# Sixteen small bias transfers in place of one, a private bias buffer, and a reordered program start in a two-block transformer kernel

## The chip, the cores and the metric

The kernel runs on one core of a Trainium2 chip, as one program in one launch. The metric is the device time of that program in microseconds (us), of which lower is better. Times are medians over runs; the spread of the runs is given beside them. The profile is that of one further execution.

The engines are named as in the profile: PE is TensorE, DVE VectorE, ACT ScalarE, POOL GpSimd and SP SyncE. SP and POOL only issue transfers here. The transfers of all queues are carried out by the core's 16 DMA engines.

## The reference

The input is x, 256 tokens by 1024 features, in fp32. It goes through two blocks of two layers each. The first block is an "even" mixer (sparse and compressed attention), an MLP, a differential-attention mixer (the second mixer, called DIFF or "d" in the code) and an MLP, and ends in a norm. The second block is a pooling mixer, an MLP, a block attention with a relative-position bias (MOBA or "b") and an MLP, all with norms that are scaled and shifted by vectors computed from an input c. What the change touches is the start of the first layer and the bias of the last attention:

```python
def rms_norm(x, g):
    y = xf * lax.rsqrt(jnp.mean(xf * xf, axis=-1, keepdims=True) + NORM_EPS)
    return (y * g.astype(jnp.float32)).astype(x.dtype)
...
# first block
u = rms_norm(h, mix_norm_g[layer])
h = h + even_mixer(u, even_w_in[e], ...)          # proj = u @ w_in, rope, attentions, @ w_out
...
# second block, layer 1 (moba_attention)
bias_own = rb[t5_bucket(jnp.maximum(dist_own, 0))].transpose(2, 0, 1)[None]
logit_own = jnp.einsum('bhqd,bhkd->bhqk', qf, k_own) * scale + bias_own
logit_own = jnp.where((dist_own >= 0)[None, None], logit_own, -jnp.inf)
```

The bias depends on the distance between query and key only, so one row of 384 values for each of the 16 heads holds all of it.

## The kernel before

**Tiling.** Tokens lie in two tiles of 128 (t = 0, 1). All weights come from one array, in_stream, cut into 179 pieces of up to 128 x 2048 fp32 (1024 KB). SP loads piece n into raw[n % 4]. ACT copies it to whi in a shortened format (L416, or L586 in halves), DVE subtracts to get the rest, wlo (L700, or L811 in halves), and PE multiplies both parts with the split activations uh and ul (L1216), three matmuls for one product. The even mixer's first two pieces are 128 x 1392 (the values, L1495), and its pieces 2 to 7 are features, which are turned by rope: DVE multiplies by sine and cosine (L863, L864), PE adds the swapped half (L1518), ACT copies out to qk (L535).

**What sets the order.** Every engine runs a list written out by hand; semaphores join them. SP issues piece n + 4 when wlo of piece n is done (`lo_ready`, L342). ACT and DVE follow tables that say at which quarter of which piece a step is done. In the second mixer ACT begins piece i + 3 in quarter 1 of piece i and DVE finishes piece i + 2 in quarter 3 (hi_beside, lo_beside). The semaphore `used` counts pieces that PE has finished: DIFF is 42 (the second mixer's first piece), MLP1 is 58 (the first piece of the MLP after it).

**The start.** SP issues the two halves of x and then the first four pieces. ACT issues the constants con (2197 columns) on its own DMA queue. The norm of tile t is: square and sum (L426), square root (L431), scaling on DVE (L733), transposes on PE (L1294), gain on ACT (upper, L443), split into uh and ul on DVE (lower, L746, L747). Then come the values of the even mixer. ACT does whi of pieces 0 and 1 ahead of the gain of both tiles; DVE does wlo of both ahead of both splits.

**The bias rows.** PE gathers the bias rows into a bank (L1662), right after the first feature piece. DVE adds the mask and writes them to gb (L889), which is a view of PT, the buffer of transposed attention weights: 16 partitions by 384 values. POOL then sends gb to bias_rows in device memory, each row 128 times, with a pitch of 512 values (L365). ACT waits for that transfer (L506) before it goes on to piece 4, since it will write PT later. Much later, ahead of the last attention, POOL reads the rows back, shifted by one for each partition, into hank, 16 transfers (L398).

**POOL's list** is: small inputs, the bias rows, eight copies of the compressed keys (L372, L373), two copies of keys (L376, L377), and three times 16 pieces of w_mod (1024 KB each, L391) that DVE reduces beside the MLPs. The second 16 wait for `used` at the end of the second mixer and are used in the MLP after it.

## Time and profile before

| | us |
|---|---|
| median of 3 runs | 1263.24 |
| lowest, highest | 1263.09, 1263.97 |
| the profiled execution | 1265.12 |
| its span in the trace | 1263.2 |
| PE busy (share of the span) | 1155.1 (91%) |
| DVE busy | 807.2 (64%) |
| ACT busy | 592.3 (47%) |
| POOL busy | 45.7 (4%) |

The profiled execution took 1.9 us more than its span and 1.9 us more than the median of the runs. PE is the busiest engine by far, so what matters are the stretches in which it does not work, or works at the lower of its two clocks. The granted mean clock is 0.966 of full speed. In the span cut into 40 equal slices PE is at 4, 1 and 6 tenths in the first three and at 9 in nearly all others; the slices with low PE are those of the start, of the pooling mixer (slices 23 and 24) and the very end.

### The profile page before, as it was taken

Reading aid. Unit: us, or ns where it says so; the run is one execution under the profiler, and the core shown is the slowest. Engines: PE = TensorE matmul, PEld = TensorE weight load, DVE = VectorE, ACT = ScalarE, POOL = GpSimd, SP = SyncE. Lnnn points to the kernel's source line nnn. Section 1 sums busy time; section 2 is a strip of 40 time slices with the busy share of each in tenths; the row PEclk is TensorE's granted clock in tenths of the full one; section 3 lists DMA queues with packets and bytes.
Section 4 is the critical chain, followed back from the end, with each engine's and each line's share of the span. In section 5 each row is a group of like instructions: output and inputs, shape, how many; then the busy total and the mean of one; then the engine's idle time right before and its main releaser. Section 6 shows DMA issues by size and latency. Waiting matters only on the chain.

```text
span 1263.2 us, 18055 instructions
## 1 busy us (share of the span) xinstructions
PE 1155.1 (91%) x7384; PEld 1015.3 (80%) x7384; DVE 807.2 (64%) x1287; ACT 592.3 (47%) x914; POOL 45.7 (4%) x88
## 2 busy tenths in 40 slices
PE   4169999999999999899999849999999998999997
PEld 4167675999998877699999649999978987999996
DVE  4035734787777666787777686877775556655554
ACT  5023534634445556564344545444446454644342
POOL 1010000000000000000000000000002000000000
PEclk9679999999999999999999969999999999999999
DMA  7852403797773433569777334977735434455530
GB/s 267 122 138 71 167 27 149 297 354 276 272 293 134 167 104 130 200 254 351 276 273 277 119 133 155 359 276 279 298 134 180 154 133 150 168 199 180 187 134 34
DMA packets 35810, 248.57 MB, mean 197 GB/s; under 512 B 4304, under 2 KB 4320, under 8 KB 6928
## 3 DMA queue, kind: packets, MB, share of 16 engines
q1 hardware_dynamic: 26352, 188.61, 40.3%
q0 software_dynamic: 9232, 57.69, 13.8%
q8 instruction: 59, 0.97, 0.3%
q10 hardware_dynamic: 144, 1.12, 0.2%
q14 instruction: 23, 0.19, 0.0%
HBM read 242.55 MB, written 4.19 MB: 195 GB/s over the span
## 4 chain that ended last, share of the span: by engine, by line
PE 80%; DVE 9%; ACT 4%; issue 4%; DMA 3%; POOL 0%; DVEq 0%; ACTq 0%; POOLq 0%
PE bank L1216 67%; DMA bias_rows<-PT 3%; PE bank L1398 2%; PE bank L1632 2%; PE bank L1423 1%; DVE wlo L700 1%; PE bank L1615 1%; ACT vo L426 1%; DVE x L720 1%; DVE wlo L811 1%; PE bank L1447 1%; PE bank L1446 1%; PE bank L1445 1%; DVE work L718 1%; PE bank L1696 1%
## 5 line engine op out<-in xcount | busy, mean ns | idle before, releaser
L700 DVE TENSOR_TENSOR wlo<-raw,whi 128x2048 fp32r<-128x2048 f32 (+2 forms) x143 | 324.6, 2274 | 138.0 <-ACT whi L416 137.9
L1216 PE MATMUL bank<-uh,whi 128*128 128x256 f32 x1272 | 369.6, 291 | 36.4 <-ACT vo L522 36.4
L1216 PE MATMUL bank<-ul,whi 128*128 128x256 f32 x1272 | 361.4, 284 | 0.0
L1216 PE MATMUL bank<-uh,wlo 128*128 128x256 f32 x1272 | 361.4, 284 | 0.0
L416 ACT ACTIVATE whi<-raw 128x2048 fp32r<-128x2048 f32 (+2 forms) x143 | 270.5, 1896 | 38.9 <-DMA bias_rows<-PT 37.8
L1216 PEld LDWEIGHTS bank<-uh,whi 128*128 128x128 f32 x1272 | 245.4, 193 | 44.8 <-issue 42.5
L1216 PEld LDWEIGHTS bank<-ul,whi 128*128 128x128 f32 x1272 | 245.5, 193 | 4.4 <-issue 2.2
L1216 PEld LDWEIGHTS bank<-uh,wlo 128*128 128x128 f32 x1272 | 245.2, 193 | 0.0
L1216 PE MATMUL bank<-whi,hh 128*128 128x512 f32 x544 | 214.0, 393 | 0.0
L1216 PE MATMUL bank<-wlo,hh 128*128 128x512 f32 x544 | 212.4, 390 | 0.0
L1216 PE MATMUL bank<-whi,hl 128*128 128x512 f32 x544 | 211.8, 389 | 0.0
L1216 PEld LDWEIGHTS bank<-whi,hl 128*128 128x128 f32 x544 | 102.1, 188 | 22.0
L1216 PEld LDWEIGHTS bank<-whi,hh 128*128 128x128 f32 x544 | 102.4, 188 | 20.5 <-issue 1.2
L1216 PEld LDWEIGHTS bank<-wlo,hh 128*128 128x128 f32 x544 | 102.4, 188 | 18.8 <-issue 0.2
L474 ACT ACTIVATE hh<-work 128x512 fp32r<-128x512 f32 x56 | 35.4, 632 | 173.3 <-PE bank L1216 173.3
L470 ACT ACTIVATE work<-bank 128x512 f32<-128x512 f32 x56 | 33.5, 598 | 174.0 <-PE bank L1216 174.0
L762 DVE CUSTOM_DVE_ANT_0 qk<-qk,cb 128x1024 f32<-128x1024 f32 x96 | 113.2, 1222 | 0.0
L1216 PE MATMUL bank<-whi,uh 128*128 128x256 f32 (+2 forms) x256 | 90.3, 353 | 19.8 <-DVE ul L747 10.5
L1216 PE MATMUL bank<-whi,ul 128*128 128x256 f32 (+2 forms) x256 | 86.8, 339 | 0.0
L1216 PE MATMUL bank<-wlo,uh 128*128 128x256 f32 (+2 forms) x256 | 86.7, 339 | 0.0
L776 DVE TENSOR_TENSOR work<-work 128x512 f32<-128x512 f32 x56 | 38.7, 691 | 74.5 <-ACT work L470 74.5
L1216 PEld LDWEIGHTS bank<-whi,uh 128*128 128x128 f32 x256 | 52.0, 203 | 26.7 <-issue 16.8
(211 smaller groups left out, 1185.7 us busy)
## 6 DMA issues: line engine op xcount, KB each, us to landing
raw<-in_stream SPq DMA_DIRECT2D x176, 1024.0 KB, 4.9
qk<-in_w_mod POOLq DMA_DIRECT2D x48, 1024.0 KB, 5.9
bias_rows<-PT POOLq DMA_DIRECT2D x1, 3072.0 KB, 33.0
u<-bias_rows POOLq DMA_DIRECT2D x16, 128.0 KB, 2.7
raw<-in_stream SPq DMA_DIRECT2D x2, 696.0 KB, 12.5
con<-in_con ACTq DMA_DIRECT2D x1, 1098.5 KB, 6.9
x<-in_x SPq DMA_DIRECT2D x2, 512.0 KB, 8.1
vo<-in_fin_g POOLq DMA_DIRECT2D x2, 512.0 KB, 4.9
```

Source lines behind the costliest of these rows:

```text
L416: nc.scalar.activation(whi[:, c % RING, 0:w], raw[:, n % RING, 0:w], ACT.Copy).then_inc(hi_ready, 1)
L426: nc.scalar.activation(o_[:, t, 512 * h:512 * h + 512], x[:, t, 512 * h:512 * h + 512], ACT.Square, accum_out=ss[:, 2 * t + h:2 * t + h + ...
L470: nc.scalar.activation(work[:, s % 2, :], bank[s % 2][:, :], ACT.Relu).then_inc(relu_done, 1)
L474: nc.scalar.activation(hh[:, s % 2, :], work[:, s % 2, :], ACT.Square).then_inc(hh_done, 1)
L700: nc.vector.tensor_tensor(wlo[:, c % RING, 0:w], raw[:, raw_index(c) % RING, 0:w], whi[:, c % RING, 0:w].bitcast(fp32), ALU.subtract).then ...
L718: link(nc.vector.tensor_tensor(work[:, i, :], bank[acc_of(e)[2 * t + h]][:, :], gate[:, 512 * h:512 * h + 512], ALU.mult))
L720: nc.vector.tensor_tensor(xs, work[:, i, :], xs, ALU.add).then_inc(x_ready, 1)
L762: ins = nc.vector.tensor_tensor_reduce(out=stage[j][:, r, :], in0=stage[j][:, r, :], in1=cb[:, :], scale=1.0, scalar=0.0, op0=ALU.mult, op ...
L776: nc.vector.tensor_tensor(work[:, 2 + s % 2, :], work[:, s % 2, :], work[:, s % 2, :], ALU.mult)\
L1216: ins = mm(out, st, mv, start=start and i == 0, stop=stop and i == 2, skip_group_check=True)
L1398: ins = mm(bank[3 + c][:, c0:c1], qk[rows_, qb, 128 * t:128 * t + 128], qk[rows_, kb, 0:c1 - c0], start=True, stop=True)
L1632: ins = mm(bank[acc_of(1)[2 * t + h]][:, :], oT[c][:, k, 128 * t:128 * t + 128], w[:, k, 512 * h:512 * h + 512], start=c == 0 and k == 0, ...
```

## The change

Three things are changed.

1. The constants are laid out anew: the identity, the gain vectors and other vectors first (337 columns, C_EARLY), the rest behind (1860 columns). SP loads the first part between the two halves of x, and the rest between weight pieces 1 and 2, with a semaphore of its own (in_late). ACT no longer issues a transfer.
2. At the start ACT computes a square root of 1 as its first instruction. ACT then does whi of piece t just ahead of the gain of tile t, and DVE wlo of piece t just ahead of the split of tile t.
3. gb is a buffer of its own. ACT no longer waits for the bias transfer. POOL sends the rows in 16 transfers of one row each (192 KB: 384 values, 128 times), and transfer h waits until PE has used DIFF + h pieces. They stand between the first and the second 16 pieces of w_mod. The wait ahead of hank is for all 16.

```diff
@@ constants
-C_VEC = C_MASK + 384
+C_ID, C_VEC = 0, 128
+C_EARLY = C_VEC + V_PE + 32
+C_SW = C_EARLY
@@ buffers
+        gb = sb("gb", [16, 384])
-        gb = PT[0:16, 0, :]
@@ SP
                 sp.dma_start(x[:, t, :], a["x"][128 * t:128 * t + 128, :]).then_inc(in_x[t], 16)
+                if t == 0:
+                    sp.dma_start(con[:, 0:C_EARLY], a["con"][:, 0:C_EARLY]).then_inc(in_con, 16)
             for n in range(NRAW):
+                if n == 2:
+                    sp.dma_start(con[:, C_EARLY:], a["con"][:, C_EARLY:]).then_inc(in_late, 16)
@@ POOL
-            pool.wait_ge(bias_sb, 1)
-
-            pool.dma_start(bass.AP(gdram.tensor, 0, [[128 * 512, 16], [512, 128], [1, 384]]),
-                           gb[:, :].unsqueeze(1).to_broadcast([16, 128, 384])).then_inc(bias_out, 16)
-
+            pool.wait_ge(bias_sb, 1)
             for m in range(3):
                 if m == 0:
                     pool.wait_ge(plain_used, NPLAIN)
+                elif m == 1:
+
+                    for h in range(16):
+                        pool.wait_ge(used, DIFF + h)
+                        pool.dma_start(bass.AP(gdram.tensor, 128 * 512 * h, [[512, 1], [512, 128], [1, 384]]),
+                                       gb[h:h + 1, :].unsqueeze(1).to_broadcast([1, 128, 384])).then_inc(bias_out, 16)
+                    pool.wait_ge(used, LAST_OF[3] + 1)
                 else:
-                    pool.wait_ge(used, LAST_OF[(1, 3, 6)[m]] + 1)
+                    pool.wait_ge(used, LAST_OF[6] + 1)
-            pool.wait_ge(bias_out, 16)
+            pool.wait_ge(bias_out, 256)
@@ ACT
-            act.dma_start(con[:, :], a["con"]).then_inc(in_con, 16)
+
+            act.wait_ge(col_ready, 1)
+            nc.scalar.activation(std[:, 0:1], one, ACT.Sqrt)
             deviation(0)
-            hi_upto(1)
             act.wait_ge(in_con, 16)
             for t in range(NT):
+                hi_upto(t)
                 upper(0, t, vec[:, V_MIX:])
-            act.wait_ge(bias_out, 16)
@@ DVE
-            dve.wait_ge(in_con, 16)
             for t in range(NT):
                 scaled(0, t)
+            dve.wait_ge(in_con, 16)
             nc.vector.memset(kcm[:, :], 0.0)
-            lo_upto(1)
             for t in range(NT):
+                lo_upto(t)
                 lower(0, t)
             parts = ((0, 128), (128, 384))
+            dve.wait_ge(in_late, 16)
```

How the lists move is shown at two places. First ACT's list from its first instruction to the first splits; vo is where the squares go, whi the shortened weights, u the normed and gained x. Before:

```order
L496 DMA con<-in_con 128x2197
L426 ACT_TABLE_LOAD
L426 ACTIVATE vo,ss<-x 128x512 x2
L431 ACT_TABLE_LOAD
L431 ACTIVATE std<-ss,bias 128x1
L426 ACTIVATE vo,ss<-x 128x512 x2
L431 ACTIVATE std<-ss,bias 128x1
L416 ACTIVATE whi<-raw 128x1392 x2
L443 ACTIVATE u<-bank,con 128x128 x16
L416 ACTIVATE whi<-raw 128x2048 x2
```

And now (line numbers are those of the new file):

```order
L507 ACT_TABLE_LOAD
L507 ACTIVATE std<-one 128x1
L435 ACTIVATE vo,ss<-x 128x512 x2
L440 ACTIVATE std<-ss,bias 128x1
L435 ACTIVATE vo,ss<-x 128x512 x2
L440 ACTIVATE std<-ss,bias 128x1
L425 ACTIVATE whi<-raw 128x1392
L452 ACTIVATE u<-bank,con 128x128 x8
L425 ACTIVATE whi<-raw 128x1392
L452 ACTIVATE u<-bank,con 128x128 x8
L425 ACTIVATE whi<-raw 128x2048 x2
```

One of the two table loads is gone, the other stands first, and the second whi has moved behind the first eight gains.

Second, POOL's list, in which bias_rows is the array in device memory. Before:

```order
L360 DMA w<-in_cmp_w 128x2x64 x3
L365 DMA bias_rows<-PT 2048x1x384
L372 DMA u<-qk 64x256
```

And now:

```order
L378 DMA qk<-qk 64x256
L400 DMA qk<-in_w_mod 128x2048 x16
L389 DMA bias_rows<-gb 128x1x384 x16
L395 DMA vo<-in_fin_g 128x1024
L400 DMA qk<-in_w_mod 128x2048 x32
```

The one transfer of 2048 rows has become 16 of 128 rows, and they have moved from ahead of the key copies to between the first 16 pieces of w_mod and the vector fin_g.

## Rows read from the trace of the kernel before

**Rows 1.** Costliest groups of the page: busy, mean ns | idle before, its releaser.
```profile
L1216 PE MATMUL bank<-uh,whi 128*128 128x256 f32 x1272 | 369.6, 291 | 36.4 <-ACT vo L522 36.4
L416 ACT ACTIVATE whi<-raw 128x2048 fp32r<-128x2048 f32 (+2 forms) x143 | 270.5, 1896 | 38.9 <-DMA bias_rows<-PT 37.8
```

**Rows 2.** The chain of waits, 37 to 106 us: start, length, what.
```profile
37.50 32.99 DMA bias_rows<-PT
...
76.37 1.22 PE bank L1518 x2
77.59 6.28 PE bank L1216 x36
...
86.50 4.32 PE bank L1216 x36
...
105.68 0.43 PE bank L1518 x2
```

**Rows 3.** DVE in order of time: start, duration, operation [idle before].
```profile
14.97 3.33 DVE L700 TENSOR_TENSOR wlo<-raw,whi 128x1392 fp32r<-128x1392 f32 x2 [0.75 <-ACT whi L416]
18.21 0.28 DVE L746 CAST uh<-u 128x256 fp32r<-128x256 f32 x1
...
36.65 0.54 DVE L889 TENSOR_TENSOR PT<-bank,work 16x384 f32<-16x384 f32 x1 [3.20 <-PE bank L1662]
72.52 2.29 DVE L700 TENSOR_TENSOR wlo<-raw,whi 128x2048 fp32r<-128x2048 f32 x1 [35.32 <-ACT whi L416]
```

**Rows 4.** ACT in order of time, program start.
```profile
7.09 0.63 ACT L426 ACTIVATE vo<-x 128x512 f32<-128x512 f32 x1 [4.63 <-DMA x<-in_x]
...
8.44 1.28 ACT L431 ACT_TABLE_LOAD   x1
...
13.57 1.36 ACT L416 ACTIVATE whi<-raw 128x1392 fp32r<-128x1392 f32 x1 [0.76 <-DMA raw<-in_stream]
15.29 1.36 ACT L416 ACTIVATE whi<-raw 128x1392 fp32r<-128x1392 f32 x1 [0.36 <-DMA raw<-in_stream]
```

**Rows 5.** PE in order of time: the first matmul of the values.
```profile
19.10 0.63 PE L1216 MATMUL bank<-whi,uh 128*128 128x348 f32 x1 [6.40 <-DVE ul L747]
```

**Rows 6.** Stretches: PE, PEld, DVE, ACT, POOL busy, PEclk, DMA share, GB/s.
```profile
0.00:4.00 4.00, 0.00 (x0) 0.00 (x0) 0.06 (x1) 1.28 (x1) 2.94 (x9) 1.00 0.55 166
4.00:8.00 4.00, 0.00 (x0) 0.00 (x0) 0.08 (x1) 0.91 (x3) 1.56 (x3) 1.00 1.03 365
8.00:10.00 2.00, 0.00 (x0) 0.00 (x0) 0.08 (x1) 1.97 (x4) 0.00 (x0) 1.00 0.97 233
10.00:12.00 2.00, 1.24 (x6) 1.27 (x7) 1.40 (x6) 0.88 (x4) 0.00 (x0) 1.00 1.01 376
...
40.00:70.00 30.00, 0.00 (x0) 0.00 (x0) 0.00 (x0) 0.00 (x0) 0.00 (x0) 0.52 0.95 101
402.00:522.00 120.00, 113.85 (x728) 95.66 (x728) 77.87 (x187) 74.27 (x146) 0.00 (x0) 0.99 0.34 123
560.00:572.00 12.00, 12.00 (x81) 11.04 (x80) 12.00 (x15) 5.60 (x5) 1.58 (x3) 1.00 1.01 406
952.00:956.00 4.00, 3.72 (x17) 2.75 (x15) 4.00 (x3) 3.89 (x5) 3.23 (x7) 1.00 0.86 216
1261.00:1262.00 1.00, 0.00 (x0) 0.00 (x0) 0.00 (x0) 0.00 (x0) 0.00 (x0) 0.50 0.95 389
```

**Rows 7.** DMA issues of the page: count, KB each, median us from issue to landing.
```profile
raw<-in_stream SPq DMA_DIRECT2D x176, 1024.0 KB, 4.9
...
bias_rows<-PT POOLq DMA_DIRECT2D x1, 3072.0 KB, 33.0
...
con<-in_con ACTq DMA_DIRECT2D x1, 1098.5 KB, 6.9
```

**Rows 8.** Second mixer: two issues on SP's queue, and ACT's use of those pieces.
```profile
412.35 0.33 SPq L344 DMA_DIRECT2D raw<-in_stream  x1
...
423.90 2.00 ACT L586 ACTIVATE whi<-raw 128x1024 fp32r<-128x1024 f32 x2
...
483.75 0.33 SPq L344 DMA_DIRECT2D raw<-in_stream  x1
...
503.12 1.05 ACT L586 ACTIVATE whi<-raw 128x1024 fp32r<-128x1024 f32 x1
```

**Rows 9.** Either end of the second mixer: last matmul before it, POOL after it.
```profile
402.28 0.39 PE L1216 MATMUL bank<-whi,hl 128*128 128x512 f32 x1
...
529.27 0.53 POOL L386 DMA_DIRECT2D vo<-in_fin_g  x1 [158.51 <-PE bank L1216]
```

More of the change, by code:

```diff
@@ L21 @@
 LAM_INIT = 0.8 - 0.6 * math.exp(-0.3)
-C_ID, C_SW, C_TRI = 0, 128, 256
-C_COS, C_SIN, C_COSQ, C_SINQ = 384, 640, 896, 1152
-C_CORR = 1408
+C_ID, C_VEC = 0, 128
+V_MIX, V_MLP, V_MIX2, V_MLP2, V_POOL, V_C, V_SUB = 0, 16, 32, 48, 64, 72, 80
+V_BMOD = 81
+V_PE = V_BMOD + 96
+C_EARLY = C_VEC + V_PE + 32
+C_SW = C_EARLY
+C_TRI = C_SW + 128
+C_COS, C_SIN, C_COSQ, C_SINQ = (C_TRI + 128 + 256 * i for i in range(4))
+C_CORR = C_SINQ + 256
 C_HB = C_CORR + 128
@@ L30 @@
 C_MASK = C_CMPN + NT * NBLK
-C_VEC = C_MASK + 384
-V_MIX, V_MLP, V_MIX2, V_MLP2, V_POOL, V_C, V_SUB = 0, 16, 32, 48, 64, 72, 80
-V_BMOD = 81
-V_PE = V_BMOD + 96
-C_END = C_VEC + V_PE + 32
+C_END = C_MASK + 384
 QA, QI, KA, KI, QB, KC, VC, KS, KW = 0, 4, 6, 7, 8, 12, 13, 14, 15
@@ L232, in build @@
         in_x = [sem(f"in_x{t}") for t in range(NT)]
-        in_con, in_misc, in_w2, in_fin = sem("in_con"), sem("in_misc"), sem("in_w2"), sem("in_fin")
+        in_con, in_late, in_misc, in_w2, in_fin = sem("in_con"), sem("in_late"), sem("in_misc"), sem("in_w2"), sem("in_fin")
         cact_exp = sem("cact_exp")
```

## The prediction, written before the changed kernel was run

> **What bounds the kernel now.** I read the totals first: PE is busy for 91% of the span, so a gain has to come from a stretch in which PE stands still. The groups with their idle time name the one long hole that this change is aimed at: ACT waits 37.8 us for the bias transfer ahead of one whi, and PE 36.4 us for the copy that ACT makes after it [rows 1]. The chain of waits puts the 33.0 us of that transfer on the path, from 37.5 us on [rows 2]. The stretches show that in 40 to 70 us no engine works, the DMA engines are 95% busy and move only 101 GB/s, and PE's clock is granted at 0.52, its lower level of 1.2 GHz [rows 6]. DVE in order of time gives both ends of the hole: it has the bias row ready at 36.65 + 0.54 = 37.2 us and starts its next wlo at 72.52 [rows 3].
>
> **Part 1: the start.** Before, x, con and the first pieces are in flight together. I count bytes in the order in which they now queue: x's first half 524 KB (in thousands of bytes), early constants 173, x's second half 524, POOL's small inputs some 404, pieces 0 and 1 of 713 each. By the stretches the engines had moved 0.66 MB at 4 us, 2.12 at 8, 2.59 at 10 and 3.34 at 12 [rows 6]. Piece 0 was complete in that count (3.29 MB, con among it) at 11.9 us and ACT began it at 13.57 [rows 4], so 1.7 us lie between the last byte and its use. Now piece 0 ends at 2.34 MB, which is reached at 8.9 us: usable at 10.6. Piece 1 ends at 3.05 MB, at 11.2: usable at 12.9. x's first half was used at 7.09 and is now usable at about 5.1. The table load of 1.28 us after the first squares [rows 4] moves to where ACT waits for x. So the norm of tile 0 is ready some 3 us sooner and doesn't end last: piece 0 does. From it: whi 10.6 to 12.0 (1.36), wlo to 13.7 (half of 3.33), the first split, and PE 0.89 us after the split's start, as before (19.10 - 18.21) [rows 3, 5]: 14.6 us. PE starts **4.5 us** sooner. Before, wlo of both pieces (3.33 us) stood ahead of that split; the second now stands behind the four splits, at 16.4 to 18.1, and PE needs it after 12 matmuls and eight transposes, at about 19: hidden with 1 us to spare; a late piece 1 would cost what exceeds it. The late constants (952 KB) push back pieces 2 and 3 by 2.3 us at 404 GB/s, but these are loaded by about 20 us, when ACT is still at the gain of tile 1: nothing. If byte order doesn't decide landing (three queues share the engines unevenly), the gain is down to 2.5 us, if it is the table load and x that count, up to 5.5.
>
> **Part 2: the hole.** Without the wait on the transfer, DVE goes from the bias row straight to wlo of piece 4, as soon as whi is there. ACT is free for it at 28 us (32.7 before, less 4.5), so whi is done at 30.1. DVE has the bias row at 37.2 - 4.5 = 32.7 and starts wlo there, 39.8 us sooner than 72.5. What is late next is the rope of the first feature piece: from the start of that wlo to the swap on PE it was 76.37 - 72.52 = 3.85 us [rows 2, 3], so the swap is at 36.5. PE meanwhile does 12 matmuls of the next piece and waits some 3 us. Then the swap and 36 matmuls took 7.5 us at the lower clock (76.37 to 83.87); at full clock a swap of that width takes 0.43 and 36 matmuls 4.32 [rows 2]. The piece ends at 41.25 instead of 83.87. In sum **42.6 us**: 4.5 from the start, 35.3 from the hole, 2.8 from the clock. Weights aren't late: two pieces that were idle in the ring are loaded, and the rest follows DVE as before. The compressed-key copies on POOL's queue, which stood behind the bias transfer, start with their data and aren't in the way. ACT's new first instruction and the wait for the late constants hide in waits that exist: nothing.
>
> **Part 3: the sixteen transfers in the second mixer.** This is the part whose price the trace doesn't show directly. One transfer moves 196.6 KB out of a single partition. Bounds: if it goes at the old rate, it takes 33.0 / 16 = 2.06 us [rows 7]; if a partition gives only its share of that rate, 101 / 16 = 6.3 GB/s, it takes 31 us. The rows say more. Each of 16 DMA engines read its own partition then and got 6.3 GB/s. The last output goes at 389 GB/s, 24.3 per engine, and there, too, an engine reads one partition at a time [rows 6]. Short pieces aren't the reason: the shifted bias rows come back in pieces of 1 KB at 216 GB/s, at 0.86 busy [rows 6]. So neither a partition nor an engine limits, and what does is a path that the 16 neighbouring partitions share, some four times 24 to 25 GB/s. A single partition then gives 24.3: **8.1 us** for a transfer, in which all 16 DMA engines are held. I take that, since it is the rate of a row that one engine reads.
>
> The Trainium skill has the same from the other side (SBUF — State Buffer, Door 1: The DMA port swizzle): sixteen ports of 27.2 GB/s, and partitions 0 to 15 lie on four of them. That would be 109 GB/s for the old transfer, where the trace has 101, and 7.2 us for one of the new ones. By 7.2 in place of 8.1 the middle of the sum below would be 11 us and not 19.
>
> Sixteen of 8.1 are 130 us. Transfer 0 may start when PE is through the first MLP, at 402.7, the last a piece before 529.3, at about 522 [rows 9]: 119 us. The mixer's 16 weight pieces need 1049 KB at 406 GB/s, 2.6 us each, 41 us in all; now the engines are busy for 0.34 of this stretch [rows 6]. Where two queues are both full, at 560 to 572 us, the share is 1.01 at 406 GB/s [rows 6]: an engine carries one packet at a time. If it does so while it waits for the shared path, it is 130 + 41 = 171 us of work in 119: 52 too many. Pieces come early now: one issued at 483.75 is used at 503.12, 19.4 us later, and lands after 4.8 to 4.9, a spare of about 14.6 [rows 7, 8]. Of the 52 that leaves 37 us on PE. If weight packets slip in while the path is busy, only 130 - 119 = 11 count, less than the spare: 0. I take the middle, **19 us**. The first piece has less spare (issued 412.35, used 423.90 [rows 8]) and meets three transfers at once, so waits on ACT for raw should begin there. The second w_mod pieces queue behind the last transfer, but they are needed 25 us later: nothing.
>
> **Sum.** The profiled execution: 1265.1 - 42.6 + 19 = 1241.5; the median lies 1.9 under it: 1239.6, **1240**.
>
> **Rivals.**
> *The transfers are hidden.* They take 2.06 us each, or their wait doesn't hold the engines. For it speaks that 16 x 2.06 + 41 = 74 us fit in 119, and the spare of 14.6 us. Against it speaks the rate of 101 beside 389. Time: 1263.2 - 42.6 = 1221, with 3 us either way for the start and the clock.
> *The start keeps a hole.* The stretch from 28 to 41 us needs piece 4, the early constants and the bias inputs; were one late, or the swap behind a slower chain, the change would do only part of what it says. Every idle 30 us before had all pieces loaded. With 8 us kept and the transfers hidden: 1229.
> *Slower than before.* The shared path gives less to one partition than 24 GB/s while 16 engines crowd on it, and the engines carry nothing else meanwhile. The loss 16 s + 41 - 119 - 14.6 exceeds 42.6 from s = 8.5 us for a transfer. At s = 10 it is 67 us: 1288. For it: my 8.1 is close to the point. Against: it takes both the slowest sharing and a lower rate than any row shows.
>
> **How the numbers follow.** Chances: transfers partly in the way (1224 to 1256) 0.47; hidden (1218 to 1224) 0.36; a hole kept 0.06; slower 0.08; gain cancelled to within what can be told 0.02; below 1217 0.01. The first has the largest chance, so 1240 is forecast; its own range is 1224 to 1256. The range 1217 to 1257 holds these two and the third, and leaves out about 1 in 10 for slower and a little at either end. A measurement of this kernel tells 0.2%, 2.5 us, from no change. Faster 0.90, same 0.02, slower 0.08.
>
> **What would show it.** The start: the first matmul of the values at 14.6, no second table load before the square root. The hole: no gap over 4 us on PE between 15 and 60 us, clock at full, the second rope at about 41. The transfers: 8 us or more from issue to landing, a DMA share near 1 in the second mixer instead of 0.34, ACT waiting there for raw, and a mixer some 19 us longer than 119. If a transfer lands after some 4 us and the share stays near 0.6, the hidden case is right and I am wrong by about 19 us; if landing takes 8 us and PE still doesn't wait, my step from a busy engine to a late weight is the wrong one.

## The result and the profile after

The changed kernel takes 1223.24 us (median of 4 runs, 1221.15 to 1225.44). The kernel before, timed beside it, takes 1263.61 us (4 runs, 1263.09 to 1267.39). The ratio is 0.9675 with a 95% interval of 0.9649 to 0.970: faster by 3.0 to 3.5%. The forecast was 1240 with a range of 1217 to 1257. The range held, and the sign; the point was 17 us too high. What came is the time of the rival named "the transfers are hidden", 1221 ± 3.

The profiled execution took 1221.15 us, 44.0 less than that of before. Some lines of its page: busy time of two engines; two groups that answer to [rows 1] (the wlo, matmul and whi lines are now L710, L1227 and L425); and the DMA issues that answer to [rows 7].

```profile
span 1219.4 us, 18071 instructions
...
PE 1149.8 (94%) x7384; PEld 1010.6 (83%) x7384; DVE 807.2 (66%) x1287; ACT 590.8 (48%) x914; POOL 53.2 (4%) x103
...
L1227 PE MATMUL bank<-uh,whi 128*128 128x256 f32 x1272 | 367.3, 289 | 0.0
...
L425 ACT ACTIVATE whi<-raw 128x2048 fp32r<-128x2048 f32 (+2 forms) x143 | 270.4, 1895 | 2.6 <-DMA raw<-in_stream 2.6
...
raw<-in_stream SPq DMA_DIRECT2D x176, 1024.0 KB, 4.9
...
bias_rows<-gb POOLq DMA_DIRECT2D x16, 192.0 KB, 9.3
```

The 36.4 us of PE idle ahead of the first group and the 37.8 us of ACT idle ahead of whi [rows 1] are gone. What ACT still waits for in this group, 2.6 us in all, are the first two pieces at the start. The second mixer's whi is made in halves by another line (L596); there it never waits for a load either, only once, 0.5 us, for PE. So ACT doesn't wait for a weight in the second mixer, and such waits are what the 19 us of the forecast rested on.

**The start.** ACT in order of time, which answers to [rows 4] (x used at 4.97 in place of 7.09, the table load at 0.73 in place of 8.44):

```profile
0.73 1.28 ACT L507 ACT_TABLE_LOAD   x1 [0.73 <-PEq L1889]
...
4.97 0.63 ACT L435 ACTIVATE vo<-x 128x512 f32<-128x512 f32 x1 [2.74 <-DMA x<-in_x]
...
10.57 1.36 ACT L425 ACTIVATE whi<-raw 128x1392 fp32r<-128x1392 f32 x1 [1.77 <-DMA raw<-in_stream]
...
14.84 1.36 ACT L425 ACTIVATE whi<-raw 128x1392 fp32r<-128x1392 f32 x1 [0.84 <-DMA raw<-in_stream]
```

PE's first matmul of the values, against 19.10 [rows 5]:

```profile
14.39 0.63 PE L1227 MATMUL bank<-whi,uh 128*128 128x348 f32 x1 [5.09 <-DVE ul L757]
```

**The hole.** DVE in order of time, which answers to [rows 3]: the bias row, and right behind it wlo of piece 4, which started at 72.52 before. Then the wlo of piece 1 at the start, which matters below.

```profile
16.23 1.61 DVE L710 TENSOR_TENSOR wlo<-raw,whi 128x1392 fp32r<-128x1392 f32 x1
...
31.55 0.55 DVE L899 TENSOR_TENSOR gb<-bank,work 16x384 f32<-16x384 f32 x1 [3.17 <-PE bank L1673]
32.13 2.29 DVE L710 TENSOR_TENSOR wlo<-raw,whi 128x2048 fp32r<-128x2048 f32 x1
```

The chain of waits for the same place answers to [rows 2]:

```profile
35.99 0.70 PE bank L1529 x2
36.69 4.32 PE bank L1227 x36
41.01 0.02 issue
```

The piece ends at 36.69 + 4.32 = 41.01 in place of 77.59 + 6.28 = 83.87.

**The second mixer.** Its two ends on POOL's list: the first bias transfer goes out when PE is through the first MLP, fin_g when PE is through the mixer. Then the mixer in one stretch, which answers to the sixth row of [rows 6], and the DMA queues in the same stretch (packets, MB, share of 16 engines; q0 is POOL's, q1 SP's).

```profile
360.16 0.55 POOL L389 DMA_DIRECT2D bias_rows<-gb  x1 [32.20 <-PE bank L1227]
...
485.24 0.55 POOL L395 DMA_DIRECT2D vo<-in_fin_g  x1 [5.46 <-PE bank L1227]
```

```profile
362.00:480.00 118.00, 111.47 (x722) 93.68 (x721) 77.63 (x184) 74.00 (x143) 7.88 (x15) 1.00 0.91 150
```

```profile
q0 software_dynamic: 943, 2.89, 58.8%
q1 hardware_dynamic: 2016, 14.68, 31.4%
...
raw<-in_stream SPq DMA_DIRECT2D x14, 1024.0 KB, 10.2
bias_rows<-gb POOLq DMA_DIRECT2D x15, 192.0 KB, 9.3
```

From the first transfer to fin_g the mixer takes 485.24 - 360.16 = 125.1 us. Before has no such transfer, so for a comparison both are counted from the end of the first MLP's last matmul (359.86 now, 402.28 + 0.39 = 402.67 before [rows 9]): 485.24 - 359.86 = 125.4 us, and 529.27 - 402.67 = 126.6. The DMA share rose from 0.34 to 0.91 and the weights' median landing in this stretch from 4.8 to 10.2 us, and the mixer was no longer for it.

### The profile page after: what moved, and what is told of

The parts are those of the page before. It is cut to its first block, busy times and chain, and to the rows that moved or that the text cites. A ratio compares the mean times of both kernels' runs of the same rounds, so it can differ in the third digit from the quotient of the medians.

```text
span 1219.4 us, 18071 instructions
## 1 busy us (share of the span) xinstructions
PE 1149.8 (94%) x7384; PEld 1010.6 (83%) x7384; DVE 807.2 (66%) x1287; ACT 590.8 (48%) x914; POOL 53.2 (4%) x103
## 4 chain that ended last, share of the span: by engine, by line
PE 84%; DVE 10%; ACT 4%; issue 1%; DMA 1%; SPq 0%; DVEq 0%; ACTq 0%
PE bank L1227 71%; PE bank L1409 2%; PE bank L1643 2%; DVE wlo L710 1%; PE bank L1434 1%; PE bank L1626 1%; ACT vo L435 1%; DVE x L730 1%; DVE wlo L821 1%; PE bank L1458 1%; PE bank L1457 1%; PE bank L1456 1%; DVE work L728 1%; PE bank L1305 1%; DVE ul L757 1%
## 5 line engine op out<-in xcount | busy, mean ns | idle before, releaser
L710 DVE TENSOR_TENSOR wlo<-raw,whi 128x2048 fp32r<-128x2048 f32 (+2 forms) x143 | 324.5, 2274 | 103.3 <-ACT whi L425 103.3
L1227 PE MATMUL bank<-uh,whi 128*128 128x256 f32 x1272 | 367.3, 289 | 0.0
L1227 PE MATMUL bank<-uh,wlo 128*128 128x256 f32 x1272 | 359.8, 283 | 0.0
L1227 PE MATMUL bank<-ul,whi 128*128 128x256 f32 x1272 | 359.7, 283 | 0.0
L425 ACT ACTIVATE whi<-raw 128x2048 fp32r<-128x2048 f32 (+2 forms) x143 | 270.4, 1895 | 2.6 <-DMA raw<-in_stream 2.6
L1227 PEld LDWEIGHTS bank<-uh,whi 128*128 128x128 f32 x1272 | 243.5, 191 | 8.4 <-issue 5.9
L1227 PEld LDWEIGHTS bank<-ul,whi 128*128 128x128 f32 x1272 | 243.6, 192 | 4.0 <-issue 1.9
L1227 PEld LDWEIGHTS bank<-uh,wlo 128*128 128x128 f32 x1272 | 243.5, 191 | 0.0
L1227 PE MATMUL bank<-whi,hh 128*128 128x512 f32 x544 | 214.0, 393 | 0.0
L1227 PE MATMUL bank<-wlo,hh 128*128 128x512 f32 x544 | 212.4, 390 | 0.0
L1227 PE MATMUL bank<-whi,hl 128*128 128x512 f32 x544 | 211.8, 389 | 0.0
L1227 PEld LDWEIGHTS bank<-whi,hl 128*128 128x128 f32 x544 | 102.2, 188 | 21.8
L1227 PEld LDWEIGHTS bank<-whi,hh 128*128 128x128 f32 x544 | 102.4, 188 | 20.6 <-issue 1.2
L1227 PEld LDWEIGHTS bank<-wlo,hh 128*128 128x128 f32 x544 | 102.4, 188 | 18.9 <-issue 0.2
L1227 PE MATMUL bank<-whi,uh 128*128 128x256 f32 (+2 forms) x256 | 90.5, 353 | 18.6 <-DVE ul L757 9.3
L1227 PE MATMUL bank<-wlo,uh 128*128 128x256 f32 (+2 forms) x256 | 86.8, 339 | 0.0
L1227 PE MATMUL bank<-whi,ul 128*128 128x256 f32 (+2 forms) x256 | 86.7, 339 | 0.0
L1227 PEld LDWEIGHTS bank<-whi,uh 128*128 128x128 f32 x256 | 52.1, 204 | 25.5 <-issue 16.9
```

The costliest lines, as they stand in the source:

```text
L425: nc.scalar.activation(whi[:, c % RING, 0:w], raw[:, n % RING, 0:w], ACT.Copy).then_inc(hi_ready, 1)
L710: nc.vector.tensor_tensor(wlo[:, c % RING, 0:w], raw[:, raw_index(c) % RING, 0:w], whi[:, c % RING, 0:w].bitcast(fp32), ALU.subtract).then ...
L1227: ins = mm(out, st, mv, start=start and i == 0, stop=stop and i == 2, skip_group_check=True)
```

## The experiments

Each kernel was timed beside the kernel before on its chip, whose own median differed a little from chip to chip. So the ratios are what to compare; they are ratios of the means, and differ a little from those of the medians. "After" stands twice, since it was timed again beside the last group.

| kernel | median us | before there | ratio | 95% |
|---|---|---|---|---|
| after | 1223.24 | 1263.61 | 0.9675 | 0.9649 to 0.970 |
| start only | 1265.16 | 1269.8 | 0.9967 | 0.9948 to 0.9986 |
| bias only | 1230.09 | 1269.8 | 0.9702 | 0.9674 to 0.973 |
| each transfer twice | 1300.11 | 1269.8 | 1.026 | 1.0226 to 1.0294 |
| 16 rows by 8 | 1224.20 | 1269.8 | 0.9658 | 0.9625 to 0.969 |
| far rows (on before) | 1251.80 | 1268.01 | 0.9871 | 0.9849 to 0.9894 |
| one in the mixer | 1235.58 | 1268.01 | 0.9740 | 0.9715 to 0.9765 |
| one early | 1250.09 | 1268.01 | 0.9859 | 0.9833 to 0.9884 |
| no first square root | 1221.85 | 1268.01 | 0.9635 | 0.9613 to 0.9656 |
| rows in the hole (on before) | 1323.63 | 1265.43 | 1.0461 | 1.0416 to 1.0505 |
| after again | 1222.75 | 1265.09 | 0.9663 | 0.9643 to 0.9684 |
| splits ahead | 1226.80 | 1265.09 | 0.9688 | 0.9669 to 0.9708 |
| start taken further | 1223.10 | 1265.09 | 0.9677 | 0.9656 to 0.9699 |

### The two halves of the change, each alone

Start only: the new start, with the bias rows as before.

```diff
-        gb = sb("gb", [16, 384])
+        gb = PT[0:16, 0, :]
@@ POOL, ahead of the key copies: one transfer; in the mixer: none
+            pool.dma_start(bass.AP(gdram.tensor, 0, [[128 * 512, 16], [512, 128], [1, 384]]),
+                           gb[:, :].unsqueeze(1).to_broadcast([16, 128, 384])).then_inc(bias_out, 16)
@@ ACT
+            act.wait_ge(bias_out, 16)
```

> Only the new program start; the bias rows go as before, in one transfer out of the view of PT, and ACT waits for it. Additive theory: PE begins 4.7 us sooner (19.10 to 14.39 in the two traces) and everything behind it moves as a block, the 33 us hole too, so 1263.6 - 4.7 = 1259. Rival: the hole or the clock takes the start's gain back (the transfer is issued sooner, but PE falls to its lower clock all the same): 1261 to 1263.

Bias only: gb's own buffer and the sixteen transfers as in after, with con's layout, loads and ACT's and DVE's order at the start as before.

> Only the private buffer and the sixteen transfers; the program start is as before. Additive theory: hole 35.3 us and clock 2.8 us: 1263.6 - 38.1 = 1225.5, and with the run before this one the two parts add up to the whole. Rival: the parts help each other (the start's order matters only once the hole is gone): 1223 or 1228.

The ratios are 0.9967 and 0.9702, by 1263.6 us a gain of 4.2 and of 37.7 us. Together that is 41.9, and the ratio of the whole change gives 41.1 (42.6 when it was timed again): the halves add up, within the intervals. The interval of the start alone is wide, 1.8 to 6.6 us, so it doesn't tell the additive 4.7 from its rival. With the start alone the hole stands where it stood, only sooner. In order of time, ACT of the start-only kernel, then PE of the bias-only one:

```profile
67.83 1.91 ACT L422 ACTIVATE whi<-raw 128x2048 fp32r<-128x2048 f32 x1 [39.17 <-DMA bias_rows<-PT]
```

```profile
19.25 0.63 PE L1218 MATMUL bank<-whi,uh 128*128 128x348 f32 x1 [6.47 <-DVE ul L749]
...
41.23 1.22 PE L1520 MATMUL bank<-work,con 128*128 128x256 f32 x2 [2.92 <-DVE bank L866]
```

### What a transfer of one row costs

Each transfer twice, the second to an array of its own:

```diff
+                        pool.dma_start(bass.AP(gdram2.tensor, 128 * 512 * h, [[512, 1], [512, 128], [1, 384]]),
+                                       gb[h:h + 1, :].unsqueeze(1).to_broadcast([1, 128, 384])).then_inc(bias_out, 16)
-            pool.wait_ge(bias_out, 256)
+            pool.wait_ge(bias_out, 512)
```

> Each of the sixteen transfers is sent twice, the second time into an array that nobody reads: the load in the second mixer is doubled. Theory that the engines are held and the weights' spare is what hides it: in the changed kernel they take 4.6 us of mean engine time each (58.8% of 118 us for 15), so 32 take 147 us, with 37 of weights 184 us in a mixer of 125; with a spare of 15 the mixer grows by some 44 us or more, PE waits on raw, 1265 or above. Theory that a slow transfer doesn't hold the engines: weights land within the spare, 1223 to 1226.

The mixer grew from 125 to 198 us. A row of the waits (us in total, times, the longest), a DMA row of the page and the mixer in one stretch:

```profile
ACT whi L600 <- DMA raw<-in_stream: 82.8, 12, 11.6
```

```profile
bias_rows<-gb POOLq DMA_DIRECT2D x32, 192.0 KB, 33.5
```

```profile
363.00:561.00 198.00, 141.94 (x758) 117.08 (x757) 84.33 (x197) 77.28 (x153) 16.83 (x33) 0.84 0.96 104
```

So the wait that I had forecast exists, on the engine and for the tile that I had named: with twice the transfers ACT waits 12 times for raw. The sixteen fit, thirty-two don't: the mixer lasts 198 / 32 = 6.2 us for each, weights and all. The engines were busy for 0.96 x 198 = 190 us, and 32 x 4.6 + 41 = 188, so in this run the length of the mixer is the work of the engines. It grew by 72.7 us, where I had expected 44 or more: the spare took nothing off.

Sixteen slices that each take all 16 rows 8 times, in place of one row 128 times; bytes, places and times of issue are the same:

```diff
-                        pool.dma_start(bass.AP(gdram.tensor, 128 * 512 * h, [[512, 1], [512, 128], [1, 384]]),
-                                       gb[h:h + 1, :].unsqueeze(1).to_broadcast([1, 128, 384])).then_inc(bias_out, 16)
+                        pool.dma_start(bass.AP(gdram.tensor, 512 * 8 * h, [[128 * 512, 16], [512, 8], [1, 384]]),
+                                       gb[:, :].unsqueeze(1).to_broadcast([16, 8, 384])).then_inc(bias_out, 16)
```

> The same bytes in sixteen transfers at the same places, but each takes all 16 rows, 8 times, in place of one row 128 times. Shared-path theory: 16 partitions give 101 GB/s, so a transfer lands after 4 us in place of 9.3, the DMA share in the second mixer falls from 0.91 to about 0.6 and weights land after 6 us or less in place of 10. Time: 1223 if the spare hid everything, 1 to 3 us less if late weights cost something that the trace hides. If the size of a transfer or the number of pieces sets its duration, it stays at 9 us and the share at 0.9.

The page's row, the mixer in one stretch and its queues:

```profile
bias_rows<-gb POOLq DMA_DIRECT2D x16, 192.0 KB, 4.1
```

```profile
363.00:481.00 118.00, 111.83 (x726) 94.27 (x725) 77.19 (x185) 74.25 (x146) 8.04 (x15) 1.00 0.48 150
```

```profile
q0 software_dynamic: 960, 2.95, 12.4%
...
raw<-in_stream SPq DMA_DIRECT2D x14, 1024.0 KB, 5.1
```

The same bytes need 0.124 x 118 / 15 = 1.0 us of all engines each and not 0.588 x 118 / 15 = 4.6, land in 4.1 us and not 9.3, and leave the weights at 5.1 us. The mixer takes 125.0 us either way and the kernel's ratio doesn't differ by what can be told. So in after the slow transfers cost nothing that can be told: when they are made cheap, nothing comes back. The one-early kernel below, which has no transfer in this mixer at all, says the same: 125.3 us from the first MLP's last matmul to fin_g, beside the 125.4 of after.

Rows in the hole, made from the kernel before, measures the disputed price by itself. The one transfer becomes sixteen of one row at its old place, and ACT waits for all:

```diff
-            pool.dma_start(bass.AP(gdram.tensor, 0, [[128 * 512, 16], [512, 128], [1, 384]]),
-                           gb[:, :].unsqueeze(1).to_broadcast([16, 128, 384])).then_inc(bias_out, 16)
+            for h in range(16):
+                pool.dma_start(bass.AP(gdram.tensor, 128 * 512 * h, [[512, 1], [512, 128], [1, 384]]),
+                               gb[h:h + 1, :].unsqueeze(1).to_broadcast([1, 128, 384])).then_inc(bias_out, 16)
```

> The kernel before, with sixteen transfers of one row (192 KB) at the place of the one, all issued one behind the other, and ACT waiting for all of them as it waited for the one. Nothing else is loaded in that hole, so it shows what sixteen such transfers cost when there is nothing beside them. Theory (one row has one path, the engines carry them in order, and a transfer is 7 us of that path: 9 us from issue to landing less some 2): sixteen take about 115 us where the one took 33, and the kernel is about 80 us slower than the kernel before (1345). My prediction's 8.1 us would give 130 us and 1360. Rival (the 4.6 us of mean engine time that a transfer took in the second mixer is its whole cost, so the paths of several rows work side by side): 74 us or less, 1305 or less.

ACT's group on the page, and the hole in stretches:

```profile
L417 ACT ACTIVATE whi<-raw 128x2048 fp32r<-128x2048 f32 (+2 forms) x143 | 270.6, 1897 | 98.2 <-DMA bias_rows<-PT 97.5
```

```profile
40.00:70.00 30.00, 0.00 (x0) 0.00 (x0) 0.00 (x0) 0.00 (x0) 6.02 (x12) 0.51 0.92 29
70.00:120.00 50.00, 0.00 (x0) 0.00 (x0) 0.00 (x0) 0.00 (x0) 0.00 (x0) 0.50 0.80 39
120.00:128.00 8.00, 0.00 (x0) 0.00 (x0) 0.00 (x0) 0.00 (x0) 0.00 (x0) 0.50 0.37 25
```

ACT waits 97.5 us in place of 37.8, so sixteen take 33.0 + 59.7 = 92.7 us where one took 33.0, or 5.8 us each. Neither theory said that: mine said 115, the rival at most 74. The share falls from 0.92 to 0.37 towards the end, so some engines are done while others still have bytes to move. I read it so: the engines don't go through a row in step, some are already at the next row, and several shared paths work at a time. The first of them lands after 9.3 us, but sixteen in a row don't take 16 times that. The trace doesn't show single engines, so this reading is argued and not shown.

### Is it the 16 neighbouring partitions that share a path?

Far rows, made from the kernel before: the one transfer reads 384 values from 16 partitions 8 apart.

```diff
+            pool.wait_ge(in_con, 16)
             pool.dma_start(bass.AP(gdram.tensor, 0, [[128 * 512, 16], [512, 128], [1, 384]]),
-                           gb[:, :].unsqueeze(1).to_broadcast([16, 128, 384])).then_inc(bias_out, 16)
+                           con[0:128:8, 0:384].unsqueeze(1).to_broadcast([16, 128, 384])).then_inc(bias_out, 16)
```

> This is the kernel before; only the one bias transfer is changed: it reads 384 values from each of 16 partitions that lie 8 apart (0, 8, 16 to 120, of the constants) in place of the 16 neighbouring ones of gb. Bytes, pieces and destination are the same. The output's bias rows are then other numbers. Theory (neighbouring partitions share a path on the side of the buffer): the 16 partitions lie on more paths, so the transfer goes faster than the 93 to 101 GB/s of rows 6 and 7, by up to the 203 GB/s that two reads per path would double it to: 33.0 us become about 17, and the kernel is about 16 us faster than the kernel before (ratio about 0.987). Rival (it is the 1.5 KB pieces, the writes with a pitch, or one engine reading one partition over and over that limits): the transfer stays at 33 us and the time is that of the kernel before (ratio 1.00).

The chain's row for it (start, length), and the stretch inside it:

```profile
37.98 18.97 DMA bias_rows<-con
```

```profile
42.00:54.00 12.00, 0.00 (x0) 0.00 (x0) 0.00 (x0) 0.00 (x0) 0.00 (x0) 0.50 0.98 192
```

19.0 us in place of 33.0 [rows 2], 192 GB/s in place of 101 [rows 6], and the kernel 16.2 us faster (1268.01 to 1251.8; expected 16). Sizes of pieces, destination and bytes are the same, so where the rows lie decides, and the prediction's reading that the 16 neighbours share a path is borne out. By the Trainium skill (SBUF — State Buffer, Door 1: The DMA port swizzle) partitions 0, 8 to 120 lie on eight of the sixteen ports of 27.2 GB/s, which gives an estimate of 218 GB/s; the trace has 192.

### Why sixteen, and why in the mixer

One early: own buffer and new start, the one transfer at its old place on POOL's list, ACT not waiting.

```diff
@@ POOL, ahead of the key copies (and none in the mixer)
+            pool.wait_ge(bias_sb, 1)
+            pool.dma_start(bass.AP(gdram.tensor, 0, [[128 * 512, 16], [512, 128], [1, 384]]),
+                           gb[:, :].unsqueeze(1).to_broadcast([16, 128, 384])).then_inc(bias_out, 16)
```

> The changed kernel's start and its own buffer, but the one transfer of 16 rows (3072 KB) at its old place on POOL's queue, ahead of the copies of the compressed keys, and ACT does not wait for it. It tells what the sixteen late transfers are for once the buffer is private. Theory (the key copies queue behind it): they come about 33 us after 32, at 65 us, where they are now needed before, and PE waits some 15 to 20 us there: 1238 to 1243. Rival (the keys are needed late enough): 1223, and the private buffer alone was the whole gain.

It is 1250.09, some 24 us slower than after by the ratios (0.9859 and 0.9663 to 0.9675). In the chain the copies of the compressed keys stand behind the transfer, which lands after 37.6 us; the second row is DVE in order of time:

```profile
42.48 34.48 DMA u<-qk
```

```profile
76.98 1.48 DVE L940 TENSOR_TENSOR u<-u,con 128x240 f32<-128x240 f32 x3 [23.14 <-DMA u<-qk]
```

The copies land after 32.3 to 34.5 us (4.9 in after), and DVE waits 23.1 us for them. So the private buffer alone takes less than half of the hole away; the move out of the keys' way is the rest. I had given the wait 15 to 20 us, and it was more.

One in the mixer: after, with the one transfer of 16 rows at the mixer's first piece.

```diff
-                    for h in range(16):
-                        pool.wait_ge(used, DIFF + h)
-                        pool.dma_start(bass.AP(gdram.tensor, 128 * 512 * h, [[512, 1], [512, 128], [1, 384]]),
-                                       gb[h:h + 1, :].unsqueeze(1).to_broadcast([1, 128, 384])).then_inc(bias_out, 16)
+                    pool.wait_ge(used, DIFF)
+                    pool.dma_start(bass.AP(gdram.tensor, 0, [[128 * 512, 16], [512, 128], [1, 384]]),
+                                   gb[:, :].unsqueeze(1).to_broadcast([16, 128, 384])).then_inc(bias_out, 16)
```

> The changed kernel, but with the one transfer of 16 rows (3072 KB) in place of the sixteen, begun when PE is at the second mixer's first piece. Theory (queues share the engines packet by packet, and weights slip in between): it lands after 33 to 45 us, pieces loaded beside it are some 6 us later than alone, within the spare of some 14 us, and the time is that of the changed kernel (ratio 1.000 to it, 1223). Rival (three pieces that the ring has just asked for meet it with less spare): ACT waits for raw at the first pieces of that mixer and the kernel is 3 to 10 us slower than the changed one.

The rival came: the ratio is 0.9740, 8 to 10 us slower than after. ACT waits for weights, in order of time, and in the stretch ahead of that wait the engines are full at the rate of the bias transfer alone:

```profile
393.12 2.00 ACT L595 ACTIVATE whi<-raw 128x1024 fp32r<-128x1024 f32 x2 [11.31 <-DMA raw<-in_stream]
...
398.48 1.06 ACT L595 ACTIVATE whi<-raw 128x1024 fp32r<-128x1024 f32 x1 [2.88 <-DMA raw<-in_stream]
```

```profile
362.00:384.00 22.00, 21.76 (x138) 18.92 (x137) 14.72 (x24) 12.05 (x20) 0.00 (x0) 1.00 0.95 98
```

The transfer lands after 37.1 us and takes 29 us of the engines (0.755 of 38 us), where the sixteen take 16 x 4.6 = 74, and yet the kernel is slower. The first weight piece issued in the mixer, at 370.2, lands after 22.9 us, when ACT has been waiting for it. In after the same piece landed in 4.8 us and was used 11.5 us after its issue. So what counts here is how long the other queue is kept out at a stretch, and that it is at the pieces with the least spare; no run parts the two. No run has the transfers anywhere but ahead of the key copies and in this mixer, either, so that the mixer is the best place for them isn't shown.

### The start in parts

No first square root: after without ACT's first instruction.

```diff
-            act.wait_ge(col_ready, 1)
-            nc.scalar.activation(std[:, 0:1], one, ACT.Sqrt)
```

> The changed kernel without the square root of 1 that ACT computes first, so that its table load stands between the squares and the square root of tile 0 again. Theory (piece 0 of the weights comes last at the start, at 10.57 us): nothing changes, 1223. Rival (the table load of 1.28 us is on the path): 1.3 us slower.

0.9635 against 0.9675 and 0.9663: not slower. In the profile the table load stands at 5.75 again, both square roots are done at 9.5, and ACT still waits 1.89 us until piece 0 is there at 11.39. This part of the change is worth nothing while piece 0 comes last.

Splits ahead: the new order of loads, but whi and wlo of both first pieces ahead of the norm's steps.

```diff
@@ ACT, and DVE with lo_upto in the same way
             deviation(0)
+            hi_upto(1)
             act.wait_ge(in_con, 16)
             for t in range(NT):
-                hi_upto(t)
                 upper(0, t, vec[:, V_MIX:])
```

> The changed kernel with one part of the new start undone: ACT makes whi of both first pieces, and DVE wlo of both, ahead of the norm's steps, as before; the order of the loads stays the new one. In the changed kernel piece 1 is usable at 14.84 us. Theory (the alternation keeps piece 1 off the path): wlo of piece 1 ends at about 17.9, the first split follows, and PE starts at about 18.8 instead of 14.39; part of that comes back, since PE then doesn't wait later on: 2 to 4.4 us slower than the changed kernel (ratio to it 1.0016 to 1.0036). Rival (the order of the loads alone gave the start its gain): same time as the changed kernel.

```profile
18.30 0.63 PE L1227 MATMUL bank<-whi,uh 128*128 128x348 f32 x1 [9.52 <-DVE ul L757]
```

PE starts at 18.30 and the kernel takes 1226.80 beside 1222.75. That is 4.05 us more (3.2 by the ratios), though the intervals of the ratios overlap. With 18.30 against 14.39, or 14.72 in the profile of after again, it says that most of the start's gain hangs on the alternation: the new order of the loads alone brought PE's start from 19.10 to 18.30, since the first split then waits for piece 1.

Start taken further: sixteen slices of all rows, SP's loads in the order x's first half, early constants, piece 0, x's second half, piece 1, and ACT and DVE finish tile 0 before tile 1. The main lines, without the slices, which are as above:

```diff
@@ SP
-            for t in range(NT):
-                sp.dma_start(x[:, t, :], a["x"][128 * t:128 * t + 128, :]).then_inc(in_x[t], 16)
-                if t == 0:
-                    sp.dma_start(con[:, 0:C_EARLY], a["con"][:, 0:C_EARLY]).then_inc(in_con, 16)
+            sp.dma_start(x[:, 0, :], a["x"][0:128, :]).then_inc(in_x[0], 16)
+            sp.dma_start(con[:, 0:C_EARLY], a["con"][:, 0:C_EARLY]).then_inc(in_con, 16)
             for n in range(NRAW):
+                if n == 1:
+                    sp.dma_start(x[:, 1, :], a["x"][128:256, :]).then_inc(in_x[1], 16)
@@ POOL
+            pool.wait_ge(in_x[1], 16)
@@ ACT (deviation(0) ahead of the loop is gone)
+                deviation(0, (t,))
                 hi_upto(t)
@@ DVE
+                scaled(0, t)
                 lo_upto(t)
```

> The changed kernel with the sixteen transfers cut the other way (each of all 16 rows, 8 times, and not of one row, 128 times) and with the start taken further: SP loads x's first half, the early constants, piece 0, x's second half, piece 1; POOL's small inputs wait for x's second half; ACT and DVE do the norm and the piece of tile 0 before those of tile 1. Theory (bytes ahead of piece 0 decide: 1.41 MB where there were 2.34): piece 0 is usable at some 7.5 us in place of 10.57, PE starts at 10.9 instead of 14.39 and the kernel is 3.5 us faster than the changed one (ratio to it 0.997). Rival (the norm of tile 1 and piece 1 come later, and PE only waits there instead): within 1 us of the changed kernel.

```profile
8.84 1.36 ACT L426 ACTIVATE whi<-raw 128x1392 fp32r<-128x1392 f32 x1 [2.79 <-DMA raw<-in_stream]
```

```profile
12.72 0.63 PE L1227 MATMUL bank<-whi,uh 128*128 128x348 f32 x1 [4.00 <-DVE ul L759]
...
17.97 0.43 PE L1227 MATMUL bank<-whi,uh 128*128 128x348 f32 x1 [0.35 <-DVE wlo L712]
```

A miss for the theory. Piece 0 came at 8.84 and not 7.5, so counting bytes gave too early a time here, and PE started at 12.72 and not 10.9. Of the 1.7 us against 14.39, 1.0 is left at the swap of the first feature piece, 34.98 against 35.99. Against the profile of after again (14.72, swap at 37.13) it would be 2.0 and 2.1, so one profile doesn't settle what is left. The median is 1223.10 beside 1222.75, no difference that can be told. No version tried beats after measurably.

The control, for the record:

> The changed kernel itself, timed beside the next two, so that they are compared with it on the same chip: ratio 0.9675 to the kernel before, as first measured.

## Why the prediction was right where it was right, and wrong where it was wrong

**Part 1, the start: right.** Forecast: x at about 5.1, piece 0 at 10.6, PE at 14.6. The rows have 4.97, 10.57 and 14.39. Counting bytes in the order of issue, with 1.7 us from the last byte to its use, worked for piece 0. It worked less well for piece 1: 14.84 against 12.9, two microseconds late. It cost nothing: whi of piece 1 ended at 14.84 + 1.36 = 16.20, and DVE was at the splits of tile 0 until 16.23 in any case, where the forecast had 16.4; wlo ended at 16.23 + 1.61 = 17.84, before PE needed it at about 18.9. The hit at 14.39 also has some luck in it: over the profiles of kernels with the same start, or without its first square root, PE's first matmul lies between 14.31 and 15.21.

**Part 2, the hole: right.** Forecast: wlo at 32.7, swap at 36.5 after a wait of some 3 us, the piece done at 41.25, 42.6 us in all. The rows have 32.13, 35.99 after 2.93, and 41.01: 83.87 - 41.01 = 42.9 us. The bias-only kernel (swap at 41.23) shows the hole's part without the start's. From 83.87 and from 41.01 to the end of the profiled executions are 1181.3 and 1180.1 us. So all of the gain but 1.1 us was made in the first 84 us.

**Part 3, the sixteen transfers: wrong.** The forecast had 19 us; nothing was lost. The point of 1240 is too high by this term; the range held because it was drawn wide enough for the rival. Four statements stood in it.

- *A path is shared by neighbouring partitions, and one partition gives about 24 GB/s.* The first half is borne out: the far rows went at 192 GB/s in place of 101. The second fits: the first transfer, with nothing beside it, landed after 8.7 us, which is 22.6 GB/s at the least. Beside weights the median is 9.3 and the slowest took 17.6.
- *"8.1 us for a transfer, in which all 16 DMA engines are held."* This is the step that failed. Beside the weights each transfer took 4.6 us of the 16 engines on the mean. So the work was 16 x 4.6 + 41 = 115 us in 119, and not 171: no overflow, by the prediction's own sum. Nor is 4.6 a fixed price. These two stretches hold the first transfer with nothing beside it:

```profile
360.00:364.00 4.00, 3.84 (x21) 2.87 (x20) 2.59 (x9) 2.41 (x9) 0.55 (x1) 1.00 0.86 26
364.00:368.00 4.00, 4.00 (x19) 3.27 (x19) 3.26 (x9) 4.00 (x8) 0.00 (x0) 1.00 0.72 23
```

  Their share gives 0.86 x 4 + 0.72 x 4 = 6.3 us of the engines. By that price the sum would still be 142 us in 119, and 8 us beyond the spare; it is the fall to 4.6 once other transfers are in flight that made it fit. Rows in the hole show the same fall without any weights: from 40 to 70 us 0.92 x 30 = 27.6 us for 0.87 MB, or 6.2 us for each 196.6 KB, but 4.6 us each over all sixteen (0.796 of 92 us). Which engines are held for how long, and why less when there is other work, the traces don't show. The Trainium skill's figure of 27.2 GB/s a port (SBUF — State Buffer, Door 1: The DMA port swizzle) gave the estimate of 7.2 us for a transfer, and the forecast by it would have been wrong in the same step, since the fault lay in the holding and not in the rate.
- *The spare of 14.6 us takes up what is late.* Right, and it was needed. The weights of the mixer landed in 10.2 us on the median, but four of the first six in 18.3 to 20.3. The slowest was 15.5 us late, more than 14.6, and was saved by a spare of its own that was larger: SP issued it at 374.46 and ACT used it at 396.04.

```profile
374.46 1.16 SPq L350 DMA_DIRECT2D raw<-in_stream  x1
```

```profile
396.04 1.05 ACT L596 ACTIVATE whi<-raw 128x1024 fp32r<-128x1024 f32 x1
```

  It landed at 394.8 and was used 1.2 us later: what has been gained is near an edge, and twice the transfers made the mixer 72.7 us longer.
- *"I take the middle, 19 us."* The two mechanisms gave 37 and 0, and neither gave 19. A middle is a fair number to lose little by, but it isn't a case, and I gave it the largest chance. The rival with 0.36 had a row for its weakest point: the spare was measured, and the holding of all engines wasn't.

The test that the prediction named last ("if landing takes 8 us and PE still doesn't wait, my step from a busy engine to a late weight is the wrong one") is what came. Landing took 8.7 to 9.3 us, the share was 0.91, and PE didn't wait. The weights were late; the engines had the time, and the spare covered it.

The mixer became 1.2 us shorter (126.6 to 125.4), and the transfers have no part in it: the one-early kernel, without any there, has 125.3. What goes with it is the granted clock. Before has a stretch at 0.72 (455 to 461 us), the start-only kernel one at 0.50 in the same 6 us and a mixer of 128.1, the far rows one at 0.83 (440 to 450) and 126.6; after and one early show 1.00 throughout. Why some have it stays open.

## What to carry to other kernels

A buffer that is shared with a slow transfer costs the wait for that transfer at the next writer, and giving it a buffer removes that wait, but look then at what is queued behind the transfer on its own queue: here the key copies would have kept 24 of the 41 us. Send such bytes in parts that are paced by the progress of the work beside which they run, cut so that each part spreads over all source partitions that there are (the slices left the weights' landing at 5.1 us, the single rows doubled it for nothing). When pricing a transfer against another queue, take the engines' busy share and the longest time for which the other queue is kept out, not the landing time, and hold that against the spare between landing and use. Here the share was known only from a run: measured alone, a transfer cost 6.3 us, and 4.6 in company.

## What the runs showed of the hardware that was not expected

- Sixteen transfers of one row, one behind the other with nothing else beside them, take 5.8 us each, though the first one in the mixer, alone, lands after 8.7 us. With each sent twice and weights beside them it is 6.2 us each, the weights' share included.
- Weights on SP's queue were kept out far longer by the one large transfer than by sharing the engines in turn. In the one-in-the-mixer kernel a piece issued at 370.2 us landed after 22.9 us and the one issued at 372.4 after 26.1. From 371 to 383 us all but one of the 252 packets that moved were of POOL's queue, and none was of SP's. Until 384 us the engines moved 98 GB/s, which is the bias transfer's own rate. I had expected some 6 us. What gives POOL's queue this precedence over some 12 us, the runs don't show.
